# Nearly all input-projection units in three reduced-precision passes, and the state-space scan in three vector operations per step

## The reference, cut to what is computed

```python
xn = rmsnorm(x, norm_mix)
u, q, k, v, qi, ki, wi, gl = split(xn @ w_in)          # 2048 -> 8272 columns
# q, k: norm and rope; qi, ki: rope
# prompt: index scores, exact top 64 of a row, masked attention
# sample: index scores over 2048 cached keys and 1 new one, exact top 256, gathered attention
h[t] = abar * h[t-1] + (bbar @ u[t])                   # complex, 64 groups x 64 states
y_ssm = gelu(Re(c @ h) + d * u);  y_ssm *= sigmoid(y_ssm @ w_glu)
x += (sigmoid(gl0) * (y_ssm @ w_br0) + sigmoid(gl1) * (y_att @ w_br1)) @ w_out
gate, up = split(rmsnorm(x) @ w_ffn_up);  x += (silu(gate) * up) @ w_ffn_down
```

## Time and profile before

| | |
|---|---|
| median of 3 runs | 3066.21 us (3065.42 to 3075.17) |
| the profiled execution's own time | 3065.53 us |
| its span, first to last instruction | 3063.7 us |
| mean granted TensorE clock | 0.998 |
| TensorE matmul busy | 3006.6 us, 98% |
| VectorE busy | 1956.3 us, 64% |
| ScalarE busy | 1240.4 us, 40% |
| bytes moved | 546.5 MB, 178 GB/s |

### The profile page before, as it was taken

One profiled execution on the slowest core, in us unless ns is written; L12 is line 12 of the kernel. 1 busy time (PEld: TensorE's weight loads), 2 busy tenths in 40 slices (PEclk: granted clock), 3 DMA queues, 4 the chain that ended last, 5 costly groups with the idle time before them and its releaser, 6 DMA issues. The chain is left out here.

```text
span 3063.7 us, 58940 instructions
## 1 busy us (share of the span) xinstructions
PE 3006.6 (98%) x23528; PEld 2860.5 (93%) x23528; DVE 1956.3 (64%) x3397; ACT 1240.4 (40%) x1735; POOL 253.4 (8%) x239
## 2 busy tenths in 40 slices
PE   7999999999999999999999999999999999999999
PEld 7988878999999999999989888789999999999999
DVE  7559868577656545565575697785776555456553
ACT  4443333544554333434334422335435453333432
POOL 4320000400000000000043200004000000000000
PEclk9999999999999999999999999999999999999999
DMA  6447434745555655556555573347455556555564
GB/s 249 163 153 196 144 125 137 246 168 177 198 182 181 200 170 178 179 184 206 186 188 167 156 196 127 126 147 244 167 175 199 185 178 201 170 178 182 183 208 134
DMA packets 150194, 546.47 MB, mean 178 GB/s; under 512 B 19825, under 2 KB 25073, under 8 KB 149521
## 3 DMA queue, kind: packets, MB, share of 16 engines
q1 hardware_dynamic: 137296, 507.40, 49.3%
q0 software_dynamic: 12096, 35.67, 4.6%
q10 hardware_dynamic: 640, 1.16, 0.1%
HBM read 536.95 MB, written 7.21 MB: 178 GB/s over the span
## 5 line engine op out<-in xcount | busy, mean ns | idle before, releaser
L1795 DVE TENSOR_TENSOR w_ffn_low<-ring_ffn,w_ffn_high 128x1024 fp32r<-128x1024 f32 (+1 forms) x480 | 638.7, 1331 | 456.9 <-ACT w_ffn_high L1289 456.8
L1289 ACT ACTIVATE w_ffn_high<-ring_ffn 128x1024 fp32r<-128x1024 f32 (+1 forms) x480 | 548.0, 1142 | 641.7 <-PE main L1016 641.5
L1014 PE MATMUL main<-x_ffn_high,w_ffn_high 128*128 128x264 f32 x2816 | 792.5, 281 | 0.0
L1016 PE MATMUL main<-x_ffn_high,w_ffn_low 128*128 128x264 f32 x2816 | 792.1, 281 | 0.0
L1015 PE MATMUL main<-x_ffn_low,w_ffn_high 128*128 128x264 f32 x2816 | 792.1, 281 | 0.0
L1014 PEld LDWEIGHTS main<-x_ffn_high,w_ffn_high 128*128 128x128 f32 x2816 | 527.1, 187 | 0.1
L1015 PEld LDWEIGHTS main<-x_ffn_low,w_ffn_high 128*128 128x128 f32 x2816 | 527.1, 187 | 0.1
L1016 PEld LDWEIGHTS main<-x_ffn_high,w_ffn_low 128*128 128x128 f32 x2816 | 527.1, 187 | 0.0
L1014 PE MATMUL main<-hidden_high,w_ffn_high 128*128 128x264 f32 x1408 | 396.1, 281 | 0.0
L1015 PE MATMUL main<-hidden_low,w_ffn_high 128*128 128x264 f32 x1408 | 396.1, 281 | 0.0
L1016 PE MATMUL main<-hidden_high,w_ffn_low 128*128 128x264 f32 x1408 | 396.1, 281 | 0.0
(11 more groups left out here) (378 smaller groups left out, 4804.0 us busy)
## 6 DMA issues: line engine op xcount, KB each, us to landing
ring_ffn<-in_w_up SPq DMA_DIRECT2D x352, 512.0 KB, 3.3
ring<-in_w_in SPq DMA_DIRECT2D x260, 512.0 KB
ring_ffn<-in_w_down SPq DMA_DIRECT2D x128, 704.0 KB, 4.1
ring<-in_w_br SPq DMA_DIRECT2D x64, 512.0 KB
ring<-in_w_out SPq DMA_DIRECT2D x64, 512.0 KB
w_low<-in_w_in POOLq DMA_DIRECT2D x20, 512.0 KB, 7.0
ring<-in_w_glu SPq DMA_DIRECT2D x16, 512.0 KB
out_x<-x SPq DMA_DIRECT2D x8, 528.0 KB, 5.9
```

The source lines that it names most:

```text
L1014: mm(out, wfh[:, slot, w], high[:, kk, :], start=kk == 0, stop=False)
L1016: m = mm(out, wfl[:, slot, w], high[:, kk, :], start=False, stop=kk == chunks * kts - 1)
L1289: af(wfh[:, s, 0:cols], ring_ffn[:, s, 0:cols], ACT.Copy).then_inc(high_ready, 1)
L1795: tt(wfl[:, s, 0:cols], ring_ffn[:, s, 0:cols], wfh[:, s, 0:cols].bitcast(F32), ALU.subtract).then_inc(low_ready, 1)
```

## The change

- All of units 10 to 131 are split. Of 56 to 91 those with u % 3 = 2 and 56 to 59 are split by VectorE, the other 22 are `ADDED`. 92 to 107 are split by VectorE. Of 108 to 131 those with u % 6 = 5 (113, 119, 125, 131) are split by VectorE and 20 are `ADDED`. Per layer that is 42 `ADDED` units for 10, and 80 for 65 split by VectorE.
- High parts rotate over five places from unit 56 on, later over four, with nine places in all. Gate blocks 16 to 31 go where the normed x was. The first two `w_glu` highs get a place of their own.
- The old x, for the residual, is loaded beside units 138 to 153 and not beside 112 to 127.
- A scan step is three operations: one product of 1024 elements with a table of coefficients, and two adds of 512, each waiting for the one before, on the way back too. ScalarE writes the tables with 8 copies per half (`coefficients`).
- The gathers of the second and third sequence's keys wait for unit 131 and not for units 127 and 129.

```diff
-LATE = {92: 0, 93: 1, 94: 0, 95: 1, 96: 2, 97: 3, 98: 0, 99: 2, 100: 3, 101: 0, 102: 2, 103: 3, 104: 0, 105: 2}
-BESIDE = {59: 2, 60: 0, 63: 1, 65: 2, 66: 0, 69: 1, 71: 2, 72: 0, 75: 1, 77: 2, 78: 0, 81: 1, 83: 2, 84: 0, 87: 2}
-ADDED = [60, 63, 66, 69, 72, 75, 78, 81, 84, 87]
-SPLIT = [*range(10, 56), 59, 65, 71, 77, 83, *LATE, *range(G_GLU, G_END)]
-X_AT = 112
+ADDED = [u for u in (*range(60, 92), *range(108, 131)) if (u % 3 != 2 if u < 92 else u % 6 != 5)]
+SPLIT = [u for u in (*range(10, 132), *range(G_GLU, G_END)) if u not in ADDED]
+HIGH_IN = {u: u % 4 if u < 56 or u >= 100 and u % 4 >= 2 else u % 5 if u < 100 else 5 + u % 4 for u in range(10, 118)}
+HIGH_IN |= {118: 7, 119: 3, 120: 5, 121: 6, 122: 8, 123: 3, 124: 7, 125: 5, 126: 6, 127: 8, 128: 7, 129: 5, 130: 8, 131: 7}
+X_AT = 138
...
-        gates = arena[:, 0:32 * T].rearrange("p (m t) -> p m t", t=T)
+        gates = [arena[:, (16 + m) * T:(17 + m) * T] for m in range(16)] + [xn[:, m, :] for m in range(16)]
...
-                    def evac_gates(first, count):
+                    def highs_after(done):
+
+                        while next_high < G_GLU and high_free(next_high) <= done:
+                            highs_to(next_high)
+
+                    def evac_gates(first, count, ahead=4):
                         for f in range(first, first + count):
-                            highs_to(min(2 * f + 5, ADDED[-1]))
+                            highs_to(min(2 * f + ahead, G_GLU - 1))
...
+                    def coefficients(half):
+
+                        tiles = slice(HALF * half, HALF * half + HALF)
+                        for near in (True, False):
+                            table = step_coef[half] if near else far_coef[:]
+                            for kind in range(2):
+                                power = apow[:, kind, :, tiles] if near else far_pow[:, :, kind, tiles]
+                                for c in range(2):
+                                    af(table[:, :, kind, c:ST:2], power, ACT.Copy, scale=-1.0 if kind and c else 1.0).then_inc(s5_copied, 1)
...
+                    act.wait_ge(cneg, 1)
+                    coefficients(0)
                     act.wait_ge(pi_done, 2)
                     bu(0)
...
-                    evac_gates(50, 4)
+                    act.wait_ge(units, 106)
+                    coefficients(1)
+                    evac_gates(50, 4, 5)
...
                         for j in range(attend_units(u), attend_units(u + 1)):
+                            highs_after(2 * 54 + j + 1)
...
-                    lows_to(12)
+                    lows_to(13)
...
                         if n == 8:
-                            lows_to(14)
+                            lows_to(15)
+                    lows_to(16)
...
-                    lows_to(16)
+                    lows_to(18)
...
-                        if n % 6 == 0 and n <= 24:
+                        if n % 3 == 0:
                             lows_to(59 + n)
...
-                        def fma(cur, prev, pr, pi, n):
-
-                            m1, ins = products(pw1, prev, pr, n)
-                            st.mark(ins)
-                            m2, ins = products(pw2, prev, pi, n)
-                            st.link(ins)
-                            st.link(tt(cur, cur, m1, ALU.add))
-                            st.mark(tt(cur[:, :, 0, :], cur[:, :, 0, :], m2[:, :, 1, :], ALU.subtract))
-                            st.link(tt(cur[:, :, 1, :], cur[:, :, 1, :], m2[:, :, 0, :], ALU.add))
+                        dve.wait_ge(s5_copied, 4 + 8 * (half + 1))
+
+                        def fma(cur, prev, coef, n):
+
+                            m = pw[:, 0:ST * 2 * n].rearrange("p (k m n) -> p k m n", k=2, n=n)
+                            was = prev.rearrange("p s c n -> p (s c) n").unsqueeze(1).to_broadcast([P, 2, ST, n])
+                            st.link(tt(m, was, coef.unsqueeze(3).to_broadcast([P, 2, ST, n]), ALU.mult))
+                            own, crossed = (m[:, kind].rearrange("p (s c) n -> p s c n", c=2) for kind in range(2))
+                            st.link(tt(cur, cur, own, ALU.add))
+                            st.link(tt(cur, cur, crossed[:, :, ::-1, :], ALU.add))
...
                         for j in range(CH):
                             turn()
...
                             if j < CH - 1:
+                                fma(hh[:, :, :, NC * j + 1:NC * j + NC], last, near[:, j], NC - 1)
...
-                    lows_to(55)
+                    lows_to(57)
                     dve.wait_ge(bu_copied, 32)
                     count_at(score, 0.0)
                     scan(0, bisect)
...
-                    lows_to(105)
+                    lows_to(107)
...
                     def attend(n):
 
+                        if n in (5, 15, 23):
+                            lows_to({5: 113, 15: 119, 23: 125}[n])
...
                     scan(1, attend)
                     dve.wait_ge(hs_saved, 2)
                     dve.sem_inc(scan_done, 1)
+                    lows_to(131)
                     skip(1)
```

More of the change, by code:

```diff
@@ L142, in build @@
         far = sb("far", [P, 6 * ST])
+        far_coef = sb("far_coef", [P, 3, 2, ST])
         qb = sb("qb", [P, 4, 32])
@@ L328, in build, with parted @@
         HIGH_AT = (0, KT8, 8 * T, 8 * T + KT8)
-        late_high = (whb[:, :, 0:KT8 // 2], whv[:], *(
-            whq[:, KT8 * j:KT8 * j + KT8].rearrange("p (c n) -> p c n", c=2) for j in range(2)))
+        in_high = [wih[:, at:at + KT8] for at in HIGH_AT] + [
+            whb[:, :, 0:KT8 // 2], whq[:, 0:KT8], whq[:, KT8:2 * KT8], whb[:, 1, :], wha[:]]
+        def parted(u):
+            return HIGH_IN.get(u) == 4
         def unit_w(u):
[L335 to L342, removed]
+            raw, low = ring[:, u % 6, :], wlow[:, u % 6, :]
+            if parted(u):
+                raw, low = (a.rearrange("p (c n) -> p c n", c=2) for a in (raw, low))
+            if u in HIGH_IN:
+                return raw, in_high[HIGH_IN[u]], low
+            if G_GLU <= u < G_GLU + 2:
+                return raw, wgh[:, u - G_GLU, :], low
+            at = HIGH_AT[u % 4]
+            return raw, wmh[:, at:at + KT8], low
@@ L344, in weight @@
         def weight(a, u, k):
-            return a[:, k // 4, k % 4 * P:k % 4 * P + P] if u in LATE or BESIDE.get(u) == 2 else a[:, k * P:(k + 1) * P]
+            return a[:, k // 4, k % 4 * P:k % 4 * P + P] if parted(u) else a[:, k * P:(k + 1) * P]
         def high_free(u):
-            if u in LATE:
-                return max((n + 1 for n in LATE if n < u and LATE[n] == LATE[u]), default=ADDED[-1] + 1)
-            if u in BESIDE:
-                return max((n + 1 for n in BESIDE if n < u and BESIDE[n] == BESIDE[u]), default=56)
@@ L353, in high_free @@
-            if u < 14:
-                return 0
-            if G_GLU <= u < G_GLU + 4:
-                return G_GLU - 1 if u < G_GLU + 2 else G_GLU
+            if u in HIGH_IN:
+                first = 106 if HIGH_IN[u] == 7 else 56 if HIGH_IN[u] == 4 else 0
+                return max((n + 1 for n in HIGH_IN if n < u and HIGH_IN[n] == HIGH_IN[u]), default=first)
+            if u < G_GLU + 6:
+                return 0 if u < G_GLU + 2 else G_GLU
             return u - 3
@@ L559, in _ @@
                         load(u)
+                        if X_AT <= u < X_AT + NT:
+                            k = u - X_AT
+                            sp.dma_start(x[:, k, :], (o["x"] if layer else d["x"])[:, k, :]).then_inc(x_in, 16)
                     sp.wait_ge(hs_saved, 2)
@@ L1607, in scan @@
                         for k in range(4):
                             back, ends = 1 << k, SEQ - NC
-                            pr, pi = (apow[:, c, CH - 1, tiles] if k == 0 else far_pow[:, k - 1, c, tiles] for c in range(2))
                             turn()
-                            fma(hh[:, :, :, ends + back:SEQ], hh[:, :, :, ends:SEQ - back], pr, pi, NC - back)
+                            fma(hh[:, :, :, ends + back:SEQ], hh[:, :, :, ends:SEQ - back],
+                                near[:, CH - 1] if k == 0 else far_coef[:, k - 1], NC - back)
@@ L1911, in _ @@
                             pool.wait_ge(low_added[n % 2], added_by(ADDED[n - 2]))
-                        raw = d["w_in"][layer, u - 2]
-                        g.dma_start(unit_w(u)[2], raw.rearrange("p (c n) -> p c n", c=2) if BESIDE[u] == 2 else raw,
-                                    accum_op=ALU.add).then_inc(low_added[n % 2], 16)
+                        g.dma_start(wlow[:, u % 6, :], d["w_in"][layer, u - 2], accum_op=ALU.add).then_inc(low_added[n % 2], 16)
                     pool.wait_ge(gix_ready, 1)
@@ L1934, in _ @@
                     for b in range(3):
-                        pool.wait_ge(units, 2 * 63 + 2 * b)
+                        pool.wait_ge(units, G_GLU if b else G_GLU - 6)
                         gather_keys(b)
```

84 lines of the change are left out of this document (33 added, 51 removed).

## The result

The kernel after takes 3104.66 us (median of 4 runs, 3103.22 to 3109.36) where the kernel before takes 3068.84 in the same comparison: a ratio of 1.0117, 95% interval 1.0095 to 1.0139, so 29 to 43 us more. The prediction said 3078, and 3060 to 3104. The direction was right; two thirds of the size were missed. The profiled execution of after took 3109.36 us.

The account below looks back on a forecast made before the run. VectorE was taken to set the pace of both scan stages (units 56 to 90 and 106 to 129). Terms of +6.0 us a layer, twice +12.0, on 3065.5 gave 3077.5, stated as 3078 us; range 3060 to 3104.

Parts of the forecast that it names:

- the early lows: Units 10 to 19: lows 13 and 15 made ahead of the operations that held them up, -2.3 us a layer.
- `coefficients(0)`: Eight ScalarE table copies in front of bu(0): +1.3 us a layer, between 0 and 1.6.
- units 56 to 90: First scan stage: seven more lows +7.9, half a scan +0.2, waits gone -2.5; sum +5.6 us a layer.
- unit 91: The unit after the first scan stage, between two short waits for VectorE: -0.6 us a layer.
- units 108 to 129: Stage of scan(1): three lows +3.4, half scan +0.2, waits of 1.3 and 0.3 gone; +2.0 us a layer.
- TensorE's 47 cheaper units a layer: 47 more split units save TensorE 0.66 us each, 31 us a layer; judged lost in the scan stages, where VectorE sets the pace.
- rival 3: Waits on VectorE cost nothing, so a half scan is 12 us shorter, 48 us in all: 3030 us; chance 8%.
- item 6: Units 130 and 131 save 1.3 us, but unit 132 waits for VectorE; moved loads and gathers also covered: nothing.
- Split units at 2.90 throughout: Check on the profile after: each split unit takes 2.90 us on TensorE everywhere.
- Rival 5: TensorE idles more and its clock falls; a tenth of the two stages' 112 units hit, 17 us: 3095; chance 5%.
- items 3 and 4: Units 56 to 90 at +5.6 us and unit 91 at -0.6 us a layer; lows 106 and 107 cost nothing.
- rival 1: Adding DMAs come late in the scan stages: 4.1 us a unit, 11 us a layer on top, 3100 us; chance 17%.

Follow-up runs that it names:

- i1: Kernel after with merged_high 64 bytes earlier in SBUF; 3092.74 us, ratio 1.0047 to the kernel before.
- e2: Kernel after with far_coef allocated behind xn, so that what the kernel before has, network included, is at its old place; 3106.92 us, ratio 1.0094.
- f5: Kernel before with lows 13, 15, 16 and 18 made earlier and the three-operation step in the forward scan only; 3057.65 us, ratio 0.9965.
- e3: Kernel after with 34 float32r matmuls into a free bank behind unit 90, where TensorE stood idle; 3112.97 us, ratio 1.0111 to the kernel before.
- h1: Kernel before with w_mid_high 192 bytes further on in SBUF; 3068.24 us (one run).
- e1: Kernel before with 768 bytes a partition left empty, so all allocated behind far stands 768 bytes further on; 3078.57 us, ratio 0.9997.
- g2: Kernel after with one TensorE drain per layer inside the network's first block, behind the sum of squares; 3097.42 us, ratio 1.0095 to the kernel before.
- h5: Kernel before with one TensorE drain ahead of the feed-forward network in each layer; 3078.15 us, ratio 1.0034.
- i2: Kernel after with merged_high 64 bytes earlier and unread matmuls where TensorE waits for VectorE; 3093.92 us, ratio 1.0049 to the kernel before.
- h3: Kernel after with matmuls that nobody reads wherever TensorE waits for VectorE; 3098.24 us, ratio 1.0096 to the kernel before.
- f1: Kernel after, unchanged, run again beside the other kernels of its set; 3104.62 us, ratio 1.0118 to the kernel before.

## Why the prediction was right and wrong

**Right: VectorE's part up to unit 132.** With the network's pace back (i1), the change costs 10 to 18 us, and my sum was 12. (i1 ran on a slower chip. On another slow one e2, with the slow network, cost 24 to 34.) By its own items: the early lows gave -2.4 us (-2.3); `coefficients(0)` +1.5 (+1.3); units 56 to 90 +5.8 to +6.2 (+5.6); unit 91 at full clock 3.3 us for 4.0 (-0.6); units 108 to 129 +1.5 in i1 and +2.5 in after (+2.0, from waiting and lows in scan(1)); units 130 to 132 nothing. TensorE's 47 cheaper units a layer are lost, as argued, since VectorE sets the pace and got more to do; f5, which gives VectorE less to do and leaves the units alone, wins. The rule of the Trainium skill in "VectorE: DVE Perf Modes", section "The DRAIN you can't avoid", weighed as rival 3, finds no support: the product's interval with its wait is 1.24 us and the adds' 0.73, and the half scan became no shorter than my sum.

**Wrong: the sum ended at unit 132.** The step that failed is the end of the list: item 6 closes with "nothing", no term stands for the split units and the network behind unit 132, and the check says "Split units at 2.90 throughout". That put the cost of everything later at nothing, without a reason but that the diff leaves the network's code alone. The diff moves operands of units 132 to 203, though: `w_mid_high`, `merged_low` and `merged_high` change places. Units 172 to 202 went to 2.93 us each (90.72 / 31), 0.8 us a layer, and the network behind them took over a slower pattern: 776.2 us for 768.3 in layer 0 and, from unit 203 to the end of the span, 777.0 for 768.5 in layer 1. That is 16 us, and 18 with the split units, of the 24 by which the sum fell short. The prediction read the diff's list of places as a matter of who overwrites what and not as a matter of time.

**Wrong too, and smaller: unit 91.** The step is "Unit 91, between two waits for VectorE that are short: -0.6 us". With VectorE late and TensorE early the wait ahead of it became 4.2 us in layer 0 and 3.2 in layer 1, the clock fell, and the unit took 5.6 and 5.9 us for 4.0. That is 2.3 and 2.6 us more than at full clock. Rival 5, with 5% and 17 us for a tenth of all units, came true on this scale. Where the pause was filled (e3), units 56 to 91 took 133.5 us in layer 0, 5.1 more than before, and items 3 and 4 had said 5.6 - 0.6 = 5.0.

**Where the profiled execution has its time.** The spans of after and before differ by 43.9 us, 8 more than the medians: 19.0 in units 3 to 131 of both layers, where the sum had 12.0 (unit 91 at the low clock is 4.9 of the difference), 5.1 in units 132 to 171, 18.1 from unit 172 on, and 1.7 ahead of unit 3. The 5.1 are all in layer 1, with 142.3 us for 137.0, a granted clock of 0.98 for 1.00, and a wait of 2.6 us for gathered keys for 0.7. Profiles differ there by some us whatever the kernel (f5, which has none of the change there, 138.1 and 139.9), so I don't count these 5.1 as the change's. Whether the clock costs anything in the medians isn't shown: e3 filled one pause, and its runs gained nothing.

**The checks, one by one.** Held: VectorE's waits (1.6 us, all ahead of the first count), the two step lengths, the start of unit 91. Half wrong: TensorE's waits for counts came to 8.7 us in eight units and not to over 15 in nearly every one, and an adding DMA was waited for 1.3 us once, where I had said none above 1; rival 1 had its beginnings here, but at 2.0 us a stage it decided nothing. Its price holds a slip: 20.4 us in five pitches are 4.1 a unit, 0.3 over the 3.8 and not 0.35, so 9 us a layer and 3096. Wrong: the pace of split units. Twenty adding DMAs in 218:331 of after took 52.3% of the time, 2.95 us of all sixteen engines each, where ten took 3.07 each before; their landings came later, 5.4, 7.8 and 10.3 us (least, median, longest) for 5.2, 7.0 and 8.8.

**Open.** Which rule of places makes the patterns, and by what mechanism, wasn't settled. h1 and i1 show that single moves of 192 and 64 bytes matter, e1 that moving all by 768 doesn't, g2 and h5 that a drain can flip the state either way. No run moved `merged_high` in the kernel before, which would show whether that alone makes its network slow. The time that the clock's falls cost over a whole run came out between nothing (i2 beside i1) and 6 us (h3 beside f1).

## What to carry to other kernels

Count the matmul records of a long unchanged stretch before and after a change; a pace that differs by 1% at the same clock and 100% busy can't be seen in shares, and here it cost 16 us. When a change moves operands, list the stages that read them, and those that follow without a pause. And a unit made cheaper on an engine that waits anyway gives nothing: give the engine that sets the pace less to do.

## What the runs showed of the hardware that was not expected

- One stream of identical float32r matmuls of 264 columns ran at 120.0 or at 121.3 ns a matmul, granted clock 1.00, for a whole layer's network, in the same program (g2, h5). The Trainium skill gives N ÷ 2.4 GHz + 2.5 ns for isolated matmuls in "TensorE: Matmul & The Clock Gate", section "Back-to-back issue gap", by which my estimate for 264 columns is 112.5 ns, and says that in a stream of weight loads and matmuls both set the spacing. Both paces here lie above that estimate.
- The pace of the network changed with the place of an operand that only an earlier stage reads (i1: 64 bytes, 3299 to 3336 matmuls in 400 us in both layers), and a drain of TensorE between the stages can change it to the better (g2) or to the worse (h5: +9 us).
- 4.2 us without a matmul were followed by 24 matmuls at a start-to-start time of 0.22 us; filling the pause with work that nobody reads brought 0.12 back (e3).
- The same kernel differs by 10 us from chip to chip (medians of 3067 to 3069 and of 3078 to 3079), and not in the network: there the profile of e1 on a slow chip has 768.3 us in layer 0 as before has, but 158.3 for 155.7 in units 10 to 51 and 144.0 for 137.5 in units 132 to 171.
